# PEER gate tables on one Trainium2 core: 24 expert columns from plain fp32 products to split operands, with the work on one-hot rows handed between GpSimd and VectorE

## The reference, cut to what matters

```python
expert = e1 * N_KEYS + e2
gate = jax.nn.softmax(best.astype(jnp.float32), axis=-1).astype(xc.dtype)
act = jax.nn.gelu(jnp.einsum('thkd,td->thk', u_tab[expert], xc), approximate=False)
return jnp.einsum('thk,thkd->td', gate * act, v_tab[expert])
```

## Time and profile before

| | |
|---|---|
| median of 3 runs | 1744.89 us (1742.8 to 1745.3) |
| profiled execution, its own time | 1743.69 us |
| its span | 1741.9 us |
| granted TensorE clock, mean | 0.991 |
| PE, PEld busy | 97%, 77% |
| DVE, ACT, POOL busy | 60%, 42%, 28% |

### The profile page before, as it was taken

One profiled execution on the slowest core, in us unless ns is written; L12 is line 12 of the kernel. 1 busy time (PEld: TensorE's weight loads), 2 busy tenths in 40 slices (PEclk: granted clock), 3 DMA queues, 4 the chain that ended last, 5 costly groups with the idle time before them and its releaser, 6 DMA issues.

```text
span 1741.9 us, 25939 instructions
## 1 busy us (share of the span) xinstructions
PE 1682.1 (97%) x9914; PEld 1348.9 (77%) x9914; DVE 1042.5 (60%) x2038; ACT 738.0 (42%) x1031; POOL 488.7 (28%) x247
## 2 busy tenths in 40 slices
PE   7999989999999999999999999999999999899997
PEld 4888656879999999777788888888877898555454
DVE  2789766630995888877776777667554742422213
ACT  2353354434445566433345445554548540221221
POOL 1466200657786999110000000000043620000000
PEclk9999999999999999999999999999999999999999
DMA  9477221334543222455555555555613336599995
GB/s 380 164 276 274 103 97 49 130 137 167 196 174 141 73 97 80 182 179 189 192 176 186 192 193 184 182 188 205 280 55 139 112 130 269 197 429 427 427 427 217
DMA packets 33349, 343.79 MB, mean 197 GB/s; under 512 B 3952, under 2 KB 4592, under 8 KB 5360
## 3 DMA queue, kind: packets, MB, share of 16 engines
q1 hardware_dynamic: 31968, 339.78, 51.5%
q10 hardware_dynamic: 1296, 2.84, 0.4%
HBM read 340.51 MB, written 2.10 MB: 197 GB/s over the span
## 4 chain that ended last, share of the span: by engine, by line
PE 87%; DMA 5%; DVE 3%; ACT 3%; issue 1%; POOL 0%; SPq 0%; DVEq 0%; ACTq 0%; PEldq 0%
PE psY L991 20%; PE psD L653 13%; PE psD L726 12%; PE psD L977 6%; PE psD L731 6%; PE psD L1226 5%; PE psY L951 5%; PE psD L967 3%; PE psD L979 3%; PE psD L1235 3%; DMA ring<-in_w_in 2%; DMA arena<-in_experts 2%; PE psY L834 2%; ACT arena L1349 1%; PE psY L653 1%
## 5 line engine op out<-in xcount | busy, mean ns | idle before, releaser
L991 PE MATMUL psY<-ring_r,work_r 128*128 128x512 f32 x1536 | 365.9, 393 | 1.8 <-issue 1.8
L991 PEld LDWEIGHTS psY<-ring_r,work_r 128*128 128x128 f32 x1536 | 280.1, 188 | 71.7 <-issue 10.5
L1349 ACT ACTIVATE arena<-psD 128x512 f32<-128x512 f32 (+5 forms) x182 | 124.6, 688 | 353.0 <-PE psD L731 117.7
L1349 ACT ACTIVATE ring_r<-ring 128x1024 fp32r<-128x1024 f32 x188 | 192.7, 1056 | 172.0 <-PE psY L991 115.2
L977 PE MATMUL psD<-xh_r,ring_r 128*128 128x512 f32 x480 | 171.3, 397 | 0.0
L2221 DVE TENSOR_TENSOR ring_r<-ring,ring_r 128x1024 fp32r<-128x1024 f32 x128 | 156.3, 1221 | 14.6 <-ACT ring_r L1349 14.3
L1847 POOL TENSOR_TENSOR ring_r<-ring,work_r 128x1024 fp32r<-128x1024 f32 x48 | 116.1, 2428 | 169.5 <-ACT work_r L1349 169.5
L1876 POOL TENSOR_TENSOR h_lo<-xh,work_r 128x256 fp32r<-128x256 f32 x8 | 6.8, 884 | 487.9 <-DVEq L2337 487.9
L979 PE MATMUL psD<-xh_r,ring_r 128*128 128x256 f32 x480 | 134.6, 280 | 0.0
L977 PEld LDWEIGHTS psD<-xh_r,ring_r 128*128 128x128 f32 x480 | 90.2, 188 | 21.6
L2216 DVE TENSOR_TENSOR ring_r<-ring,ring_r 128x1024 fp32r<-128x1024 f32 x60 | 73.5, 1225 | 40.9 <-ACT ring_r L1349 40.9
(11 more groups left out here) (406 smaller groups left out, 3557.0 us busy)
## 6 DMA issues: line engine op xcount, KB each, us to landing
ring<-in_tables SPq DMA_DIRECT2D x60, 1024.0 KB, 4.9
arena<-in_experts SPq DMA_DIRECT2D x30, 2048.0 KB, 20.1
ring<-in_w_in SPq DMA_DIRECT2D x18, 2048.0 KB, 9.4
ring<-in_experts SPq DMA_DIRECT2D x18, 2048.0 KB, 17.8
ring<-in_early_v SPq DMA_DIRECT2D x34, 1024.0 KB, 4.9
ring<-in_w_mod SPq DMA_DIRECT2D x12, 2048.0 KB, 9.3
ring<-in_early_u SPq DMA_DIRECT2D x11, 2048.0 KB, 8.4
ring<-in_mid_u SPq DMA_DIRECT2D x12, 1024.0 KB, 5.0
```

The source lines that it names most:

```text
L991: last = nc.tensor.matmul(psY[:, t * D + h * 512:t * D + (h + 1) * 512], wgt[:, b, t * P:(t + 1) * P], v[:, h * 512:(h + 1) * 512], start= ...
L1349: return nc.scalar.activation(dst, src, f, **kw)
```

## The change

1. Mid columns use split operands. ACT rounds them (mid_round, two in the early phase, then up to three ahead of PE), the high parts lie in mid_hi (three places), POOL makes the rests (mid_rest), PE does PARTS = 24 products per column. h_lo is copied from top_lo by POOL during the last 18 early columns; h_hi is not overwritten any more, so POOL's restoring of both goes.
2. one_a is made by DVE alone: eight tensor_scalars per turn, each a comparison of 128 elements of the iota (a copy in psY) with the token's e1, times the token's gate. The five rows of one_b read that iota too.
3. Mid activations go to gate_all for tokens whose gates are not made yet and stay in psY for the earlier ones. gate_early covers the finished mid columns as well, gates_out the rest; mid_gate multiplies for the earlier tokens, once per pair of columns, inside the stage.
4. The loops of DVE and POOL in this stage are written out. The semaphore counts of later parts move accordingly. LEAD is 24 products.

The diff, cut (indentation shortened; left out are the counts of later waits, the semaphore a_same and declarations):

```diff
@@ -43,7 +43,8 @@
...
 MID = 24
-LEAD = 12
+LEAD = 24
+PARTS = 3 * D // P
...
@@ -93,7 +94,19 @@
 def mid_done(n):
-    return LEAD + (MID * K - LEAD) * n // (T // 8) if n else 0
+    return LEAD + (MID * PARTS - LEAD) * n // (T // 8) if n else 0
+def mid_pairs(n):
+    return mid_done(n + 1) // (2 * PARTS)
+def mid_rounded(n):
+    return min(MID, mid_done(n) // PARTS + 3)
...
@@ -377,11 +395,11 @@
...
                     for r in (ring, ring_r))
-hi_slot, hi_plain = (r[(SPLIT0 + 2) % RING] for r in (ring_r, ring))
+hi_slot = ring_r[(SPLIT0 + 2) % RING]
 u_hi, v_hi = ([hi_slot[:, (2 * i + j) * D:(2 * i + j + 1) * D] for j in range(2)] for i in range(2))
-mid_act = [a.rearrange("p (e t) -> p e t", e=8)
-           for a in (xh[:, 0].rearrange("p k t -> p (k t)"), hi_plain[:, 0:2048], col_slot[3])]
+mid_hi = [col_lo[3][:, 0:D], col_lo[3][:, D:2 * D], hi_slot[:, 0:D]]
+iota_wide = psY[:, 0:P]
...
@@ -561,10 +579,7 @@
...
     for u in range(4):
-        if u < 3:
-            sp.wait_ge(mid_used, MID // 2 - 2 + u)
-        else:
-            sp.wait_ge(mid_gated, 2)
+        sp.wait_ge(mid_used, min(MID // 2 - 2 + u, MID // 2))
...
@@ -941,17 +956,29 @@
     def mid_step(i):
-        col, k = divmod(i, K)
+        col, part = divmod(i, PARTS)
         m, j = divmod(col, 2)
-        if j + k == 0:
-            pe.wait_ge(col_loaded[m % 3], 16 * (m // 3 + 1))
-            if m >= 2:
-                pe.wait_ge(mid_ready, m - 1)
-        at = j * D + k * P
-        last = nc.tensor.matmul(psY[:, 1024 + 512 * (m % 2) + j * T:1024 + 512 * (m % 2) + (j + 1) * T],
-                                col_slot[m % 3][:, at:at + P], hT[:, k, :], start=(k == 0), stop=(k == K - 1))
-        if j == 1 and k == K - 1:
-            last.then_inc(mid_used, 1)
+        if part == 0:
+            pe.wait_ge(u_hi_ready, MID_AT + col + 1)
+            if col == 0:
+                pe.wait_ge(h_split, 3 * K)
+            if j == 0 and m >= 2:
+                pe.wait_ge(mid_gated, m - 1)
+        if part == 2 * K:
+            pe.wait_ge(u_lo_ready, MID_AT + col + 1)
+        ps = psY[:, 1024 + 512 * (m % 2) + j * T:1024 + 512 * (m % 2) + (j + 1) * T]
+        if part < 2 * K:
+            k, which = divmod(part, 2)
+            nc.tensor.matmul(ps, mid_hi[col % 3][:, k * P:(k + 1) * P], (h_hi, h_lo)[which][:, k, :],
+                             start=(part == 0), stop=False)
+        else:
+            k = part - 2 * K
+            last = nc.tensor.matmul(ps, mid_weights(col_lo, col)[:, k * P:(k + 1) * P], h_hi[:, k, :],
+                                    start=False, stop=(k == K - 1))
+            if k == 0:
+                last.then_inc(split_done, 1)
+            if j == 1 and k == K - 1:
+                last.then_inc(mid_used, 1)
...
@@ -1002,7 +1029,7 @@
         expert_v(n + EARLY, c % 2, col_lo[(PRE + c) % 4][:, D:2 * D], False, last_column)
-    pe.wait_ge(mid_ready, MID // 2)
+    pe.wait_ge(mid_gated, MID // 2)
...
@@ -1535,6 +1562,14 @@
...
             act.sem_inc(sc_ready, 1)
+    def mid_round(col):
+        m = col // 2
+        act.wait_ge(col_loaded[m % 3], 16 * (m // 3 + 1))
+        if col >= 3:
+            act.wait_ge(split_done, MID_AT + col - 2)
+        fn(mid_hi[col % 3], mid_weights(col_slot, col), ACT.Copy).then_inc(u_hi_ready, 1)
...
@@ -1542,6 +1577,9 @@
...
             weight_round(SPLITS + 2 * n + 4)
+        if n == TOPU // 2 - 2:
+            for col in range(2):
+                mid_round(col)
...
@@ -1562,29 +1600,36 @@
         fn(b, b, ACT.Relu, scale=-1.0, bias=1.0).then_inc(b_ready, 1)
-    def gates_out(it, h, after=gb_done):
-        act.wait_ge(after, it * 2 + (h + 3))
-        fn(by_tok[:, bass.ds(it * 16 + 8 * h, 8), TOPU:],
-           psD_all[:, 1024 * h:1024 * (h + 1)].rearrange("p (t e) -> p t e", t=8)[:, :, TOPU:],
+    def gates_out(n, after=gb_done):
+        h, first = n % 2, TOPU + 2 * mid_pairs(n)
+        act.wait_ge(after, n + 3)
+        fn(by_tok[:, 8 * n:8 * n + 8, first:],
+           psD_all[:, 1024 * h:1024 * (h + 1)].rearrange("p (t e) -> p t e", t=8)[:, :, first:],
            ACT.Copy).then_inc(gate_copied, 1)
-    def mid_gelu(m):
+    def mid_gelu(m, n):
         act.wait_ge(mid_used, m + 1)
-        fn(mid_act[m // 4][:, 2 * (m % 4):2 * (m % 4) + 2, :].rearrange("p e t -> p (e t)"),
-           psY[:, 1024 + 512 * (m % 2):1536 + 512 * (m % 2)], ACT.Gelu).then_inc(mid_ready, 1)
+        ps = psY[:, 1024 + 512 * (m % 2):1536 + 512 * (m % 2)].rearrange("p (e t) -> p e t", e=2)
+        fn(ps[:, :, 0:8 * n], ps[:, :, 0:8 * n], ACT.Gelu)
+        fn(gate_all[:, TOPU + 2 * m:TOPU + 2 * m + 2, 8 * n:], ps[:, :, 8 * n:], ACT.Gelu).then_inc(mid_ready, 1)
...
     act.wait_ge(x_stored, 16)
-    done = 0
+    done, rounded_to = 0, 2
...
         it, h = divmod(n, 2)
-        while done < MID // 2 and 2 * K * (done + 1) <= mid_done(n + 1):
-            mid_gelu(done)
-            done += 1
+        for col in range(rounded_to, mid_rounded(n)):
+            mid_round(col)
+        rounded_to = max(rounded_to, mid_rounded(n))
+        for m in range(done, mid_pairs(n)):
+            mid_gelu(m, n)
+        done = mid_pairs(n)
         if n + 1 < T // 8:
-            gates_out(it, h)
+            gates_out(n)
...
@@ -1846,33 +1891,34 @@
...
                                 ALU.subtract).then_inc(u_lo_ready, 1)
+        if c >= MID_AT - 18 and c % 2 and c < MID_AT - 2:
+            k = (c - (MID_AT - 18)) // 2
+            nc.gpsimd.tensor_copy(h_lo[:, k, :], top_lo[:, k, :]).then_inc(h_split, 1)
+    def mid_rest(col):
+        pool.wait_ge(u_hi_ready, MID_AT + col + 1)
+        nc.gpsimd.tensor_tensor(mid_weights(col_lo, col), mid_weights(col_slot, col),
+                                mid_hi[col % 3].bitcast(F32), ALU.subtract).then_inc(u_lo_ready, 1)
+    for col in range(2):
+        mid_rest(col)
     pool.wait_ge(pick_ready, 2)
-    with pool.Fori(0, T // 16) as it:
-        for h in range(2):
-            pool.wait_ge(gb_done, it * 2 + (h + 1))
-            e2 = pick[:, 1, bass.ds(it * 16 + (8 * h + DVE_B), 8 - DVE_B)].rearrange("p (t a) -> p t a", a=1)
-            nc.gpsimd.tensor_tensor(one_b[:, h, DVE_B:], iota8[:, 0:8 - DVE_B],
-                                    e2.broadcast_to([P, 8 - DVE_B, P]), ALU.subtract).then_inc(b_diff, 1)
-            pool.wait_ge(a_same, it * 2 + (h + 1))
-            g = pick[:, 2, bass.ds(it * 16 + 8 * h, 8)].rearrange("p (t a) -> p t a", a=1)
-            nc.gpsimd.tensor_tensor(one_a[:, h], one_a[:, h], g.broadcast_to([P, 8, P]),
-                                    ALU.mult).then_inc(a_ready, 1)
-    pool.wait_ge(x_stored, 16)
-    pool.wait_ge(mid_used, MID // 2)
-    pool.wait_ge(mid_gated, 6)
-    for k in range(K):
-        pool.wait_ge(v_done, 12 + 2 * k)
-        nc.gpsimd.tensor_copy(h_hi[:, k, :], hT[:, k, :]).then_inc(h_hi_ready, 1)
-        pool.wait_ge(v_done, 13 + 2 * k)
-        pool.wait_ge(h_hi_ready, 2 * K + k + 1)
-        nc.gpsimd.tensor_tensor(h_lo[:, k, :], hT[:, k, :], h_hi[:, k, :].bitcast(F32),
-                                ALU.subtract).then_inc(h_split, 1)
+    rested = 2
+    for n in range(T // 8):
+        pool.wait_ge(gb_done, n + 1)
+        e2 = pick[:, 1, 8 * n + DVE_B:8 * n + 8].rearrange("p (t a) -> p t a", a=1)
+        nc.gpsimd.tensor_tensor(one_b[:, n % 2, DVE_B:], iota8[:, 0:8 - DVE_B],
+                                e2.broadcast_to([P, 8 - DVE_B, P]), ALU.subtract).then_inc(b_diff, 1)
+        upto = mid_rounded(n - 1) if n else 2
+        for col in range(rested, upto):
+            mid_rest(col)
+        rested = max(rested, upto)
+    for col in range(rested, MID):
+        mid_rest(col)
...
     for k in range(K):
-        pool.wait_ge(h_hi_ready, 3 * K + k + 1)
+        pool.wait_ge(h_hi_ready, 2 * K + k + 1)
...
@@ -2181,37 +2227,54 @@
     by_tok = gate_all.rearrange("p e t -> p t e")
-    def gate_early(it, h, after=gate_copied):
-        dve.wait_ge(after, it * 2 + (h + 3))
-        a = by_tok[:, bass.ds(it * 16 + 8 * h, 8), 0:TOPU]
-        tt(a, psD_all[:, 1024 * h:1024 * (h + 1)].rearrange("p (t e) -> p t e", t=8)[:, :, 0:TOPU], a,
+    def gate_early(n, after=gate_copied):
+        h, end = n % 2, TOPU + 2 * mid_pairs(n)
+        dve.wait_ge(after, n + 3)
+        if mid_pairs(n):
+            dve.wait_ge(mid_ready, mid_pairs(n))
+        a = by_tok[:, 8 * n:8 * n + 8, 0:end]
+        tt(a, psD_all[:, 1024 * h:1024 * (h + 1)].rearrange("p (t e) -> p t e", t=8)[:, :, 0:end], a,
            ALU.mult).then_inc(early_gated, 1)
-    def of_token(what, at, n):
-        return pick[:, what, bass.ds(at, n)].rearrange("p (t a) -> p t a", a=1).broadcast_to([P, n, P])
-    def gate_rows(it, h):
-        dve.wait_ge(gb_done, it * 2 + (h + 1))
-        tt(one_a[:, h], iota8, of_token(0, it * 16 + 8 * h, 8), ALU.is_equal).then_inc(a_same, 1)
-        tt(one_b[:, h, 0:DVE_B], iota8[:, 0:DVE_B], of_token(1, it * 16 + 8 * h, DVE_B),
-           ALU.is_equal).then_inc(b_same, 1)
+    def mid_gate(m, n):
```

(60 more changed lines are left out.)

1 line of the change is left out of this document (removed).

## The result

| | before | changed |
|---|---|---|
| median, first comparison | 1745.25 us (5 runs) | 1751.03 us (5 runs, 1750.46 to 1753.28) |
| ratio | | 1.0033, 95% interval 1.0018 to 1.0047 |
| median, beside the last experiments | 1745.72 us (18 runs) | 1750.29 us (8 runs), ratio 1.0024, interval 1.0014 to 1.0035 |
| profiled execution: own time, span | 1743.69, 1741.9 | 1751.47, 1749.7 |
| gate stage, first mid product to first v product | 142.13 | 147.10 |

The change makes the kernel slower by 0.24 to 0.33%, 4 to 6 us. The forecast was 1752.0, most of it from a stage 7.9 us longer. The stage is 4.97 us longer. The remaining 2.8 us of the 7.8 by which the two spans differ lie outside: 1.45 us were there before the stage began (567.81 against 566.36), 1.4 us come behind it.

A forecast was written before the change was run, and what follows sets the result against it. The prediction took a serial POOL and ACT cycle in the gate stage as the bound: 150 us against 142.1, +7.9 - 0.3 = +7.6, or +7.1 with b_diff at 0.98, giving 1752.0 us for the median, range 1743 to 1760.

The forecast's parts named there:

- the likeliest case: Gate stage: the POOL and ACT cycle decides, 150 us against 142.1, the kernel slower at 1752.0 us; chance 0.53.
- DVE's sum: Gate stage: DVE's operations add up to 142 us before the last table, 145 with PE's tail.
- DVE alone: Gate stage set by DVE's work only: 145.3 us, 3.2 us longer than PE's old time.
- b_diff: POOL's 384-element subtraction in each gate-stage turn: 0.95 to 1.0 us, bounds 0.69 and 1.8, against 1819 ns before.
- the ring: Gate-stage turns with a new column: POOL's b_diff, ACT's square, relu and rounding, POOL's rest in series, 5.5 us a turn.
- rival 3: Gate stage: b_diff keeps 1.8 us because of slow broadcast reads, 6.3 us a turn, some 1772 us; chance 0.06.
- rival 1: Gate stage: DVE alone bounds, the POOL and ACT cycle has slack; +3.2 - 0.3, 1747.8 us; chance 0.18.
- 1 us where ACT and DVE hold each other up: Gate stage: DVE's product waits for ACT's copy behind rounding and relu; 1 us added to the stage.
- Rival 2: Gate stage: PE stays the bound, -13.8 with +1.3 for a longer tail, 1732.4 us, faster; chance 0.13.
- two prices: Gate stage: tensor_scalar at 0.26 us or less and b_diff far under its lower bound, for PE to stay the bound.
- The tail: End of the gate stage, from the last gate to the first v product: 3.8 us.
- The 0.3 us from POOL's and DVE's vanished work: First v columns behind the gate stage: removed POOL operations on h and a DVE product gain 0.3 us at most.

The follow-up runs named there:

- one_scalar: Changed kernel with the gate's factor left out of DVE's row one-hots (one scalar, no multiplication); stage 145.14 us, median 1748.66 us, ratio 1.0021 against before.
- both: Changed kernel without the gate's factor in the row one-hots and with POOL's rests one turn later; stage 132.21 us, median 1734.91 us, ratio 0.9938 against before.
- pool13: Changed kernel with one or three row one-hots a turn on POOL, rests one turn later, PE's gap filled; stage 131.99 us, median 1733.77 us, ratio 0.9927 against before.

## Why the prediction was right, and where its sizes were off

The forecast was 1752.0 (slower, 0.69); measured 1751.03 and 1750.29. Both the direction and the mechanism of the likeliest case held; several of its terms were off.

- **DVE's sum.** Each piece held: tensor_scalar 0.32 from start to start (0.323 forecast), the 640 elements 812 ns (0.83), the product at 528 elements 1.21 us from start to start (1.19; 709.80 to 711.01), the sum up to there 142.0 us busy against 142. With its part of the tail DVE is busy 145.8 of the 147.1; "DVE alone" was put at a stage of 145.3. The second per-partition scalar with its multiplication does cost time: one_scalar's compare, without the two, is 341 ns for 401. The estimate of 258 ns by the table of the Trainium skill's "VectorE: DVE Perf Modes", section on the TRN2 errata, is not what this form takes. (258 is a whole duration, to be set beside 401; the prediction set it beside 0.323, a distance from start to start.)
- **b_diff, the term mis-sized.** I took 0.95 to 1.0 us, it is 0.829, nearer to my lower bound. The ring is then 5.33, not 5.5 (its terms as written add up to 5.56). With 22 x 0.17 = 3.7 us less the ring's sum of 149 would be 145.3, and one_scalar, where DVE has slack and the ring alone is left, measures 145.1. The 150 of the forecast would be 146.3; it measures 147.1. That the 1.8 us of before were time behind DVE's operation with two SBUF inputs, as read from the earlier trace rows, held, and rival 3 is out.
- **Which of two bounds.** I let the ring decide and kept "DVE alone" as rival 1. The runs show neither alone: without DVE's excess the stage is 145.1, without the ring 145.9, with both 147.1, without both 132.2. I had the ring 4 to 5 us above "DVE alone"; they are 0.8 apart, in the other order. The term "1 us where ACT and DVE hold each other up" stood for what the two cost each other: it is 1.2 us on top of the longer one, 2.0 on top of the ring. That shortening either would give next to nothing I had not said.
- **Waits, as announced.** ACT for POOL 44.5 us (over 40), POOL for ACT's rounding 57.5 (over 50), a turn of 4.6 us on average. PE's idle time is 14 us, where I had said some 20: the stage is shorter, and PE is busy 133 us instead of 126.4.
- **Rival 2, PE stays the bound.** Did not happen, for the reason given: two prices had to be wrong at once. both and pool13 pay both prices down and land at 132, with 1734 to 1735 us for the kernel where rival 2 said 1732.4.
- **The tail** from the last gate to the first v product took 3.44 us against 3.8.
- **Not foreseen: the clock.** I looked at the longer gap as idle time only. It lets the clock fall, and filling it gives 2.8 us back in the median.
- **h_lo's copies** cost nothing that shows. In the 120 us of early-u ahead of the stage PE has no idle time in the changed kernel (the window's columns as above):

```profile
440.00:560.00 120.00, 120.00 (x1003) 120.00 (x1002) 101.48 (x409) 60.62 (x70) 100.49 (x49) 1.00 0.50 182
```

- **The 0.3 us from POOL's and DVE's vanished work behind the stage** was too little: it is 1.5, by the start of the 401st v product in the six profiles without a fall behind the gap. I had read one wait of PE's loader in the first v products; most of POOL's operations come later.
- **The total is partly luck.** In the profiled execution a stage 2.4 us too long in the sum (7.4 against 4.97) and vanished work 1.2 us too small stand on one side. On the other, outside the forecast, stand the fall behind the gap (1.4), the later falls (1.4 net) and the late start of the stage (1.45). They cancel, and the total is 1 us off in the first comparison and 1.7 beside the last experiments.
